# One yield at the head of `sb_work`: the side steps of stick breaking stand one dense slab later

## The reference, cut to what matters

```python
def stick_breaking_attention(q, k, v):      # 8 heads of 64, blocks of 128 queries
    ...
        z = jnp.einsum('bhtd,bhsd->bhts', qb, kb) * scale
        causal = jnp.arange(q1)[None, :] < jnp.arange(q0, q1)[:, None]
        log_beta = jax.nn.log_sigmoid(z)
        log_1m_beta = jnp.where(causal, log_beta - z, 0.0)
        tail = lax.cumsum(log_1m_beta, axis=3, reverse=True) - log_1m_beta
        w = jnp.where(causal, jnp.exp(log_beta + tail), 0.0)
        outs.append(jnp.einsum('bhts,bhsd->bhtd', w.astype(v.dtype), v[:, :, :q1]))
...
def hybrid_mixer(...):
    proj = h @ w_in
    ...
    merged = g[:, :, 0] * (o_a @ w_br_sb) + g[:, :, 1] * (o_b @ w_br_gla) + g[:, :, 2] * (o_c @ w_br_ca)
    return merged @ w_out
```

## Time and profile before

| what | value |
|---|---|
| runs | 1545.79, 1546.23, 1547.57 us; median 1546.23 |
| span of the profiled execution | 1544.4 us; no other time is given for that execution |
| TensorE busy | 1500.5 us, 97% of the span, 13934 matmuls |
| VectorE, ScalarE, GpSimd busy | 555.6 us (36%), 430.9 us (28%), 83.0 us (5%) |
| chain that ended last, by engine | TensorE 84%, DMA 11%, VectorE 2%, GpSimd 2% |
| DMA | 480.38 MB, mean 311 GB/s |

### The profile page before, as it was taken

The page is one execution under the profiler, slowest core; times in us unless marked ns, Lnnn a source line. Parts: engine busy times, 40 slices in busy tenths (PEclk is TensorE's granted clock), DMA queues, the critical chain, the costliest instruction groups (busy, mean ns, idle before and its releaser), DMA issues.

```text
span 1544.4 us, 30813 instructions
## 1 busy us (share of the span) xinstructions
PE 1500.5 (97%) x13934; PEld 937.8 (61%) x13934; DVE 555.6 (36%) x672; ACT 430.9 (28%) x551; POOL 83.0 (5%) x126
## 2 busy tenths in 40 slices
PE   8999999999999999999999999999999999998877
PEld 7788888788888887887335353353433533534224
DVE  5755576655567655666400101011010110010101
ACT  6557654544445567554000000000000000000000
POOL 5211100000002111001000000000000000000000
PEclk9999999999999999999999999999999999999999
DMA  7555454665665555678999999999999999999996
GB/s 275 178 152 166 148 166 152 229 188 175 204 189 183 177 147 155 213 291 313 418 398 405 420 426 430 428 427 428 428 427 430 429 426 428 426 431 427 428 428 252
DMA packets 86242, 480.38 MB, mean 311 GB/s; under 512 B 11296, under 2 KB 13408, under 8 KB 64096
## 3 DMA queue, kind: packets, MB, share of 16 engines
q1 hardware_dynamic: 84480, 474.67, 79.3%
q0 software_dynamic: 1632, 3.74, 0.8%
HBM read 477.34 MB, written 1.05 MB: 310 GB/s over the span
## 4 chain that ended last, share of the span: by engine, by line
PE 84%; DMA 11%; DVE 2%; POOL 2%; issue 1%; ACT 0%; SPq 0%; DVEq 0%; POOLq 0%
PE pa L2128 26%; PE ps L2128 18%; PE pa L1998 13%; PE pa L2000 12%; PE pa L1999 12%; DMA exp_raw<-in_moe_slabs 11%; DVE w_lo L1292 1%; DMA w_raw<-in_w_mem_kv 1%; POOL hrs L805 1%; POOL head_gains L734 0%; PE ps L1914 0%; PE ps L2301 0%; PE ps L2122 0%; PE pa L2033 0%; PE ps L2278 0%
## 5 line engine op out<-in xcount | busy, mean ns | idle before, releaser
L2128 PE MATMUL pa<-exp_raw,xf 128*32 128x512 f32 (+1 forms) x5104 | 492.1, 542 | 19.5 <-DMA exp_raw<-in_moe_slabs 17.0
L2128 PEld LDWEIGHTS pa<-exp_raw,xf 128*32 128x32 f32 x5104 | 163.7, 110 | 325.7 <-issue 267.1
L1292 DVE TENSOR_TENSOR w_lo<-w_raw,w_hi 128x1024 fp32r<-128x1024 f32 x226 | 274.2, 1232 | 121.8 <-ACT w_hi L930 112.9
L930 ACT ACTIVATE w_hi<-w_raw 128x1024 fp32r<-128x1024 f32 (+1 forms) x228 | 236.9, 1053 | 146.3 <-PE pa L2000 144.8
L2128 PE MATMUL ps<-exp_raw,hf 128*32 128x256 f32 x4384 | 246.0, 383 | 10.0 <-DMA exp_raw<-in_moe_slabs 8.4
L1998 PE MATMUL pa<-w_hi,r 128*128 128x512 f32 x600 | 239.8, 400 | 1.2 <-DVE r L1327 1.1
L2000 PE MATMUL pa<-w_hi,r 128*128 128x512 f32 x600 | 233.9, 390 | 0.0
L1999 PE MATMUL pa<-w_lo,r 128*128 128x512 f32 x600 | 233.9, 390 | 0.0
L1859 DVE TENSOR_TENSOR hs<-pa,hs 128x768 f32<-128x768 f32 (+3 forms) x32 | 23.7, 742 | 584.2 <-ACT hs L1255 584.2
L2128 PEld LDWEIGHTS ps<-exp_raw,hf 128*32 128x32 f32 x4384 | 144.5, 111 | 114.6 <-issue 13.0
L1255 ACT ACTIVATE hs<-pa 128x768 f32<-128x768 f32 (+3 forms) x32 | 20.4, 637 | 661.0 <-PE pa L2128 661.0
(11 more groups left out here) (280 smaller groups left out, 816.3 us busy)
## 6 DMA issues: line engine op xcount, KB each, us to landing
exp_raw<-in_moe_slabs SPq DMA_DIRECT2D x82, 3072.0 KB, 33.0
exp_raw<-in_moe_slabs SPq DMA_DIRECT2D x87, 1024.0 KB, 8.2
w_raw<-in_w_in SPq DMA_DIRECT2D x104, 512.0 KB, 4.4
w_raw<-in_ff_w_gate_up SPq DMA_DIRECT2D x44, 512.0 KB, 4.5
w_raw<-in_ff_w_down SPq DMA_DIRECT2D x22, 512.0 KB, 4.2
w_raw<-in_w_mem_kv SPq DMA_DIRECT2D x16, 512.0 KB, 5.3
w_raw<-in_w_out SPq DMA_DIRECT2D x16, 512.0 KB, 4.2
w_raw<-in_w_br_sb SPq DMA_DIRECT2D x8, 512.0 KB, 3.7
```

Of the source, the lines that this page charges most:

```text
L930: act.activation(dst, raw, ACT.Copy).then_inc(hi_ready, 1)
L1292: dve.tensor_tensor(dst, raw, hi.bitcast(F32), ALU.subtract)\
L2128: return pe.matmul(dst, a, b, start=start, stop=stop, skip_group_check=True)
```

## The change

`sb_work` gets one `yield` before its loop, on all four engines. Its first call now does nothing, and each of its steps stands one call of `side()`, that is one dense slab, later than before.

```diff
@@ POOL
             def sb_work(l):
+                yield
                 for c in range(SB_HEADS // 2):
                     k = 4 * l + c
                     pool.wait_ge(sb_uu, k + 1)
```

## The result

| | before | after |
|---|---|---|
| median of the runs, us | 1546.50 (1545.72 to 1547.57, 6 runs) | 1551.05 (1550.19 to 1552.89, 6 runs) |
| ratio, 95% interval | | 1.0031 [1.0019, 1.0042] |
| span of the profiled execution, us | 1544.4 | 1548.2 (timed at 1550.19) |

The change makes the kernel 4.55 us slower, 0.31%. The forecast was +2.15 us and its range ended at 1550.8: the sign was right, the time lies outside the range.

A forecast was written before the change was run, and what follows sets the result against it. TensorE was taken to bound the mixer, the weight stream the expert stage. −1.65 + 1.90 + 1.90 = +2.15 us, added to the median 1546.23, gave 1548.4 us, range 1545.8 to 1550.8.

The forecast's parts named there:

- The start: First scores of stick breaking in layer 0: TensorE's wait for kT goes, −1.65 us; layer 1 had none, 0.
- The middle: Stick-breaking steps between start and end: moved evacuations and value products stay covered by TensorE's dense work, costed at nothing.
- The end: Before GLA's first matmuls, TensorE waits for VectorE's subtraction (L1560) on the fourth pair's value product: +1.90 us per layer.
- The rival of a longer chain, with a drain of ScalarE: ScalarE before the fourth pair's exponential takes longer: 1550.7 us with one more split, 1553.5 with drains; chance 0.18, drain 0.02.
- 1 to 1 to the end: A shift of the mixer moves the expert stage's weight stream and the kernel's end by as much.
- The clock: Rival: TensorE's clock falls in the new gaps, once in each layer, +3.4 us more, 1551.8 us; chance 0.02.
- The price of a fall: TensorE's dense work behind a new gap loses 1.7 us, half of 3.4 us at the lower clock level.

The follow-up runs named there:

- start_filled: Kernel before plus seven idle matmuls in TensorE's wait for the turned tokens r at layer 0's start; 1546.93 us, +0.26 on before.
- k_first: Kernel before with VectorE evacuating kT ahead of the splits of mem_v's slabs 2 and 3; 1546.18 us, −0.53 on before.
- drain_alone: Kernel before, nothing moved, plus a TensorE wait for the fourth pair's evacuation right behind its value product; 1551.91 us, +5.13 on before.

## Why the prediction was wrong

- **The start, −1.65 us: right.** 1.70 measured. The scores were forecast at 70.53; 70.97 less the 0.40 by which this execution already ran late is 70.57. None in layer 1.
- **The middle, nothing: right.** The fourth pair's scores stand 1.39 us later than before (140.81 against 139.42), the first pair's 1.43.
- **The end, +1.90 in each layer: right, 0.15 too long.** The forecast left the 1.70 us won at the start out of its times, so they are read 1.30 earlier (1.70 less the 0.40). Then L1553 was due at 153.87 and came at 153.84, the exponential at 154.91 and 154.89, L1560 at 159.02 and 158.99. Only the hand-over, from VectorE's end to TensorE's start, was shorter, 0.11 us and not 0.22. VectorE's two splits do decide, not the product.
- **The rival of a longer chain, with a drain of ScalarE: did not come.** The exponential is within 0.02 us of its forecast. A table load of 1.28 us at 148.21 is followed at once at 149.50. The Trainium skill, "ScalarE: Activation LUTs", section "What ACT_TABLE_LOAD costs", gives a drain of about 1380 ns with each switch to a different set; the rows on the new path show none.
- **1 to 1 to the end: right.** +3.80 at layer 1's second GLA step, at the first expert matmul and at the end of the span.
- **The clock: the step that failed.** The sum had no term for it, and the rival got a chance of 0.02 because "the stretch 65 to 70 us, with the old wait of 1.58 us in it, kept 1.00". That row could not bear it, for two reasons. It is one execution, and start_filled shows a fall behind that very wait. And the stretch ends 0.46 us after the scores start (69.54), before a fall would show: in start_filled it reads 1.00 as well, and only 70 to 75 us reads 0.66. What the runs showed in its place is a fall of 1.59 us behind layer 1's new gap.
- **The price of a fall: right.** 1.7 us forecast, 1.59 measured (in two traces of other kernels 3.2). That the rival's time of 1551.8 lies 0.75 from the result is in part luck: it has one fall in each layer, and only one of the three profiled executions of the changed kernel has that.
- **The gap's length.** The new gap is longer than the wait that the prediction took for its like: from the last dense matmul to the next 4.20 us (156.38 to 160.58), with the value product, the wait and a_up in between, against 2.83 at the wait for kT in before (67.57 to 70.40). But length alone does not sort the falls: gaps of 2.21 us (k_first, 27.24 to 29.45) and 2.85 (start_filled, 67.66 to 70.51) fell, and drain_alone's of 2.97 did not.

The three profiled executions of the changed kernel have one, two and two falls that before's does not have. By the first of them the sum is 1.79 + 1.59 + 0.40 = 3.8; with the second fall the other two stand at +5.5 and +5.0 at the first expert matmul (744.98, 744.50), and the median's +4.55 lies between.

Shown are the two gaps, their length, the falls behind them, and that a filler takes layer 1's fall away (5 of 5 open, none of 2 filled in the changed order). That it does so in layer 0 (1 of 5 open, none of 2 filled) is argued from the run times. Left open is why layer 1's gap fell in each trace and layer 0's in one; no run changed what stands ahead of a gap at equal length.

## What to carry to other kernels

Price an added wait on TensorE twice: its own length, and a spell at the lower clock behind it, with a chance to be read from more than one execution; a trace in which a gap kept its clock is one throw. Where the wait can't be removed, idle matmuls in a free bank kept the clock in all eight filled gaps that the traces show, but they leave the wait itself standing, and in start_filled's trace a fall came behind the next open wait. The late first scores were better served by moving two instructions on one engine (k_first: −0.53 us, within the noise; with the filler −1.46) than by moving a whole branch's steps on four (+4.55).

## What the runs showed of the hardware

The granted clock fell behind waits of TensorE of 1.6 to 1.8 us at four places (30, 70, 160 and 613 us), in some executions and not in others, and the dense matmuls behind them started 0.43 us apart instead of 0.23. A stretch that ends soon after a wait need not show the fall: in the changed kernel's profile 609 to 613 us, with the wait in it, reads 1.00, and 613 to 617 reads 0.57. The Trainium skill, "TensorE: Matmul & The Clock Gate", section "What's actually happening", says that the monitor's window is free-running and does not start over with the kernel, so that the point of change varies from run to run. The 1 of 5 in layer 0 agrees with that; the 5 of 5 in layer 1 would not have been read from it.
